# One hybrid decoder trunk on one NeuronCore: the attention loop written out as a stream of 64 steps, with projection and output projection placed inside it

## What is computed

```python
def nsa_mixer(h, pos, w_in, q_norm, k_norm, ..., w_out):
    q, k_c, v_c, k_s, v_s, k_w, v_w, g = jnp.split(h @ w_in, cuts, axis=-1)
    q = partial_rope(rms_norm(q.reshape(B, S, G, HP, dh), q_norm), pos)
...
    p_c = masked_softmax(s_c, mask_c)
    o_c = jnp.einsum('bghqc,bcgd->bqghd', p_c.astype(vc.dtype), vc)
...
    o = (gates[..., 0, :] * o_c + gates[..., 1, :] * o_s + gates[..., 2, :] * o_w).astype(h.dtype)
    return o.reshape(B, S, NSA_Q_WIDTH) @ w_out
...
    h = h + mix
    h = h + swiglu(rms_norm(h, ffn_norm_w[i]), ffn_w_gate[i], ffn_w_up[i], ffn_w_down[i])
```

## Time and profile before

| | us |
|---|---|
| median of three runs | 1614.51 (1613.33 to 1615.09) |
| the profiled execution | 1612.59 |
| its span from first to last instruction | 1610.8 |
| mean granted TensorE clock, as a share of 2.4 GHz | 0.982 |
| PE, DVE, ACT, POOL busy, share of the span | 94%, 53%, 39%, 16% |

### The profile page before, as it was taken

The page is one execution under the profiler, slowest core; times in us unless marked ns, Lnnn a source line. Parts: engine busy times, 40 slices in busy tenths (PEclk is TensorE's granted clock), DMA queues, the critical chain, the costliest instruction groups (busy, mean ns, idle before and its releaser), DMA issues.

```text
span 1610.8 us, 20549 instructions
## 1 busy us (share of the span) xinstructions
PE 1508.9 (94%) x7469; PEld 1217.9 (76%) x7469; DVE 853.7 (53%) x1137; ACT 630.9 (39%) x895; POOL 261.2 (16%) x289
## 2 busy tenths in 40 slices
PE   6989889778999999999999999998799999999999
PEld 5777667656788888788788867665687888887887
DVE  4556767663444444333397758789623444444222
ACT  4445655653343433323233352444223344343111
POOL 4133242301100000001000026666211000000000
PEclk9989999999999999999999999999799999999999
DMA  7200101102222222222222220111022222222222
GB/s 310 79 27 1 53 12 40 52 1 79 79 105 98 84 104 104 80 103 104 105 105 79 102 81 27 53 52 53 4 101 79 105 79 104 91 91 104 105 105 78
DMA packets 19198, 129.47 MB, mean 80 GB/s; under 512 B 2256, under 2 KB 2896, under 8 KB 4560
## 3 DMA queue, kind: packets, MB, share of 16 engines
q1 hardware_dynamic: 19008, 126.75, 21.9%
q10 hardware_dynamic: 144, 2.10, 0.4%
HBM read 126.74 MB, written 2.10 MB: 80 GB/s over the span
## 4 chain that ended last, share of the span: by engine, by line
PE 82%; issue 6%; DVE 5%; POOL 5%; ACT 2%; DVEq 0%; POOLq 0%; ACTq 0%
PE ps L354 22%; PE ps L356 22%; PE ps L355 22%; PE ps L624 3%; PE ps L607 2%; PE ps L772 2%; PE ps L587 2%; POOL Lx L1725 2%; POOL sqacc L1650 1%; PE ps L550 1%; PE ps L744 1%; PE ps L603 1%; PE ps L802 1%; DVE sm L1370 1%; PE ps L551 1%
## 5 line engine op out<-in xcount | busy, mean ns | idle before, releaser
L1152 DVE TENSOR_TENSOR wl<-wraw,wh 128x2048 fp32r<-128x2048 f32 x112 | 264.5, 2362 | 274.0 <-ACT wh L827 273.9
L354 PE MATMUL ps<-xh,wh 128*128 128x512 f32 (+2 forms) x912 | 359.3, 394 | 6.1 <-DVE xl L1162 3.4
L355 PE MATMUL ps<-xl,wh 128*128 128x512 f32 (+2 forms) x912 | 356.2, 391 | 0.0
L356 PE MATMUL ps<-xh,wl 128*128 128x512 f32 (+2 forms) x912 | 356.2, 391 | 0.0
L827 ACT ACTIVATE wh<-wraw 128x2048 fp32r<-128x2048 f32 x112 | 213.9, 1910 | 185.3 <-PE ps L356 175.5
L354 PEld LDWEIGHTS ps<-xh,wh 128*128 128x128 f32 (+2 forms) x912 | 170.8, 187 | 44.3 <-issue 4.5
L356 PEld LDWEIGHTS ps<-xh,wl 128*128 128x128 f32 (+2 forms) x912 | 170.7, 187 | 37.4
L355 PEld LDWEIGHTS ps<-xl,wh 128*128 128x128 f32 (+2 forms) x912 | 170.8, 187 | 37.0 <-issue 0.7
L354 PE MATMUL ps<-hh,wh 128*128 128x512 f32 x352 | 137.9, 392 | 4.1 <-DVE hid L1232 4.1
L355 PE MATMUL ps<-hl,wh 128*128 128x512 f32 x352 | 137.6, 391 | 0.0
L356 PE MATMUL ps<-hh,wl 128*128 128x512 f32 x352 | 137.5, 391 | 0.0
(11 more groups left out here) (262 smaller groups left out, 2491.1 us busy)
## 6 DMA issues: line engine op xcount, KB each, us to landing
wraw<-wstream SPq DMA_DIRECT2D x112, 1024.0 KB, 4.8
cw<-cw_in SPq DMA_DIRECT2D x1, 4096.0 KB, 18.9
xT<-xT_in SPq DMA_DIRECT2D x4, 512.0 KB, 8.1
xT<-xT_in ACTq DMA_DIRECT2D x1, 2048.0 KB, 8.5
out<-xT SPq DMA_DIRECT2D x8, 256.0 KB, 6.5
rows<-rows_in SPq DMA_DIRECT2D x1, 276.0 KB, 10.5
tri<-tri_in SPq DMA_DIRECT2D x1, 192.0 KB, 10.5
cmask<-cmask_in SPq DMA_DIRECT2D x1, 128.0 KB, 10.0
```

Of the source, the lines that this page charges most:

```text
L354: mm(o, wa[0], xa[0], start=start, stop=False)
L355: mm(o, wa[0], xa[1], start=False, stop=False)
L356: return mm(o, wa[1], xa[0], start=False, stop=stop)
L1152: TTo(wl[:, s, :], wraw[:, s, :], wh[:, s, :].bitcast(F32), ALU.subtract).then_inc(lo_done, 1)
```

## The change

The loop becomes 64 steps written out on every engine (`STEPS`, `place(S)`), without a seam between groups:

- **Lag.** `Pm` has three slots (`LAG = 3`). PE's `pT` comes three steps behind `qk`, and behind it in the step, where it was two; `pv` of a group reaches into steps 0, 1 and 3 of the next. `PT` gets a layout of its own by block.
- **Projection.** The 96 matmuls stand in steps 0 to 13 by the table `PROJECTED` (6, 2, 6, 2, 8, 3, 9, 12, 10, 6, 8, 8, 8, 8).
- **Turning keys and queries** is cut into six rounds of four transposes (`ROUND_AT`: steps 9, 11 and 14, and 0, 1 and 2 of the next group), each with its hi and lo part a step later; `kB1` and `kB2` have two copies. The rounds use the second halves of score banks and bank 7, so `qk` of steps 12 and 13 and of 0, 2 and 4 wait for their lo parts, and projection at step 0 waits for that of round 2.
- **Compressed branch.** Its scores move from k = 0 to step 5, its transposes from k = 1 and 5 to steps 6 and 9; the multiplication with the mask is folded into the gates once.
- **POOL** now makes the doubled copy of each normed tile (12 + 4 copies of 128x384) and stages the values.
- **Output projection.** Six of its eight input tiles are ready after group 2. Their 144 matmuls (`out_early`) stand in group 3 at steps 5, 7, ... 15 and 1 and 3 of the tail, one output tile of 18 matmuls each in bank 7; DVE adds each to `part`, a copy of x fetched during group 3. The other 48 matmuls take their weights from one extra chunk and follow at the end.
- **Norm of the first FFN.** `square` moves behind the residual, column sums and broadcast move into the FFN's second chunk, `split_lo(n0 + 2)` ahead of the mean.

```diff
-DVE_GROUP_STEPS, DVE_SCAN_STEPS = 26, 12
+STEPS = GROUPS * HP * TT
+LAG = 3
...
+ROUND_AT = {9: (1, 0), 11: (1, 1), 14: (1, 2), 0: (0, 3), 1: (0, 4), 2: (0, 5)}
+ROUND_BANK = (1, 3, 7, 1, 3, 1)
+
+PROJECTED = (6, 8, 14, 16, 24, 27, 36, 48, 58, 64, 72, 80, 88, 96, 96, 96)
+TILE_DONE = tuple(min(s for s in range(16) if PROJECTED[s] >= 24 * (tt + 1)) for tt in range(TT))
+TILE_READ = tuple(s + 1 for s in TILE_DONE)
...
+            def qk(S):
+
+                g, s, h, i = place(S)
+                w, par = (i + 1) * P, g % 2
+                if S >= 2:
+                    pe.wait_ge(expd, 2 * (S - 1))
+                if s in (0, 2, 4, 6):
+                    pe.wait_ge(qkT_lo, 6 * g + ((2, 3, 6, 6)[s // 2] if g else 6))
+                if g < GROUPS - 1 and s in (12, 13):
+                    pe.wait_ge(qkT_lo, 6 * (g + 1) + s - 11)
...
+            PV_AT = {10: (0, 0), 11: (0, 1), 12: (0, 2), 13: (0, 3), 15: (1, 0), 16: (1, 1), 17: (1, 2), 19: (1, 3)}
+
+            def step_of_attention(S):
+
+                g, s = divmod(S, HP * TT)
+                if S < STEPS:
+                    qk(S)
+                if LAG <= S < STEPS + LAG:
+                    pT(S - LAG)
+                if round_at(S):
+                    turn_keys_queries(*round_at(S))
+                if s in PV_AT and g < GROUPS:
+                    pv(g, *PV_AT[s])
+                if s + 16 in PV_AT and g:
+                    pv(g - 1, *PV_AT[s + 16])
+                if s == 5 and g < GROUPS:
+                    cmp_scoresT(g)
+                if g < GROUPS - 1:
+                    project(g, s)
+                if s == 6 and g < GROUPS:
+                    cmp_scores(g)
+                if s == 9 and g < GROUPS:
+                    cmp_transposes(g)
+                early = S - (STEPS - HP * TT) - 5
+                if early >= 0 and early % 2 == 0:
+                    out_early(early // 2)
...
-                for k in range(18):
-                    if k < 16:
-                        maxima(k)
-                    if 1 <= k <= 16:
-                        normalize(k - 1)
...
+            def step_of_attention(S):
+
+                g, s = divmod(S, HP * TT)
+                early = S - (STEPS - HP * TT) - 6
+                if early >= 0 and early % 2 == 0:
+                    add_part(early // 2)
+                if S < STEPS:
+                    maxima(S)
+                if s == 14 and g < GROUPS:
+                    o_rest(g, 0)
+                if s == 4 and g:
+                    o_rest(g - 1, 1)
+                if S and round_at(S - 1):
+                    round_lo(*round_at(S - 1))
+                if s == 7 and g < GROUPS:
+                    cmp_read(g)
+                if 1 <= S <= STEPS:
+                    normalize(S - 1)
+                if s == 7 and g < GROUPS:
+                    cmp_shift(g)
+                if s == 8 and g < GROUPS:
+                    cmp_probs(g)
+                if g < GROUPS - 1 and s in TILE_MEAN:
+                    qk_mean_square(TILE_MEAN.index(s), g + 1)
...
+                if g < GROUPS - 1 and s == 14:
+                    split_lo(n0 + 2 * g + 4)
+                if 1 <= g < GROUPS and s == 0:
+                    split_lo(n0 + 2 * g + 3)
...
+                pool.wait_ge(qk_rotated, g * 8 + 2 * (tt + 1))
+                pool.tensor_copy(qn[:, tt, :, 1, :], q6).then_inc(qk_normed, 1)
```

654 lines of the change are left out of this document (368 added, 286 removed).

## The result

The changed kernel takes **1590.76 us** (median of 4 runs, 1589.86 to 1595.0) where the kernel before takes 1614.8 on the same chip (1613.33 to 1615.25): a ratio of 0.9859, 95% interval 0.9847 to 0.987, or 24.0 us. I had forecast 1588.0, 26 to 27 us less. The profiled executions span 1588.0 us and 1610.8, a difference of 22.8.

What follows compares the result with a forecast made beforehand. PE, busy 94% of the span, bounds the kernel, so only its idle time can go. 46.1 us off less 21.1 of new waits, plus 1.2, gives 26.2: 1612.6 to 1586.4, the median 1.9 higher, so 1588; range 1568 to 1606.

Steps and rivals of the forecast that it cites:

- What goes off: Gains: 41.1 us of idle PE, 2 for group 3's slow clock, 3 for register instructions; 1.2 of further waiting at the end.
- Start, +2.8: Before the first qk: POOL's four copies of normed tiles lie wholly on PE's path, 2.8 us more.
- Seams, +2.2, +2.2, +4.5: Between groups: PE waits for DVE's lo parts, POOL's norm and exponentials; 2.2 us at the first two seams, 4.5 at the third.
- Within a group, +1.8 for round 1: Step 11: round 1 waits for tile 1's norm, ready 0 to 1.3 us late; 1.8 us for three groups.
- Compressed transposes, +2.3: Group 3, step 9: the compressed transposes wait for DVE's chain after a short step 8; 2.3 us.
- Empty pipe, +1.0: First steps of group 0: the pipe is empty, 1.0 us.
- FFN seam, +3.8: After the last early tile: DVE's splits and adds let the FFN's PE start 14.9 us behind it; 3.8 us more.
- Column sums, +0.5: In the FFN: POOL's eight sums of squares end at about 29.7, the column sums stand at 29.5; 0.5 us.
- (1): Rival: queues drift apart and fill better than walked, seams cost 0 to 1 us; 1572 us, chance 0.17.
- (2): Rival: the lag doesn't help, qk still waits for exponentials, groups 0 to 2 keep half their idle; 1596 us, chance 0.10.
- (3): Rival: DVE's full step 14 ends late, groups 0 to 2 keep 9.1 us idle each; 1609 us, chance 0.11.
- (4): Rival: written-out code costs PE instruction fetch in each of 64 steps; 1639 us at 0.8 a step, chance 0.08.

Runs made afterwards that it cites:

- e2: The changed kernel with the probabilities two steps behind the scores instead of three (LAG = 2): 1597.93 us.
- e12: The changed kernel with projection as 8 matmuls in each of steps 0 to 11 and a lag of two instead of three: 1593.3 us.
- e4: The changed kernel with the last group not filled: all eight early output tiles stand behind step 63, with their adds and splits: 1604.16 us.
- e6: The changed kernel with another projection table, 8 matmuls in each of steps 0 to 11 and none in 12 and 13: 1576.75 us.
- e9: The changed kernel with DVE's first weight split moved to step 13 and its second to step 1, projection in steps 2 and 3 adjusted: 1575.94 us.
- e10: The changed kernel with projection as 8 matmuls in each of steps 0 to 11 and DVE's first weight split in step 13 instead of 14: 1583.76 us.
- e5: The changed kernel with three edits behind step 63: last lo part before last early add, FFN start waiting for six tiles, squares pair by pair: 1590.22 us.
- e13: The changed kernel with DVE instead of POOL making the doubled copy of normed keys and queries, as before the change: 1582.22 us.

## Why the prediction was right, and where it wasn't

The sign and the mechanism were right, and the size within 3.4 us, in part by luck. I had 26.2 us between the spans and it is 22.8. By parts, forecast and measured: up to the first `qk` +2.8 and -0.5 (106.25 against 106.73); from there to the FFN -29.5 (46.1 and 1.2 off, 17.8 added) and -24.4; behind it +0.5 and +2.1. The middle part, which the change is about, was missed by 5.1; 3.3 at the start, which came from the clock ahead of the loop, made up for most of that, and that is luck. Behind the FFN's start PE's idle time is 0.6 us less than before and its busy time 2.7 more, with a granted clock of 0.92 in a stretch of the Mamba layer that had 0.95: that, too, is not a term of mine. Of the signs that I had named, the groups took 65.6, 67.3 and 66.0 us where I had 63 to 65, with PE idle 4.3 to 5.7 where I had 2 to 3.5; group 3 with its tail took 77.9 at 0.99 of the clock, inside its 70 to 80.

**What goes off** (46.1 and 1.2). PE's idle time in the stretch was 42.0 (316.0 less 274.0), and the old waits did go. e2 and e12 bring a wait for scaled probabilities back, e4 part of group 3's gaps; no run brings back the waits for copies and for bank 6. My 5 us for clock and registers were too much: PE's busy time fell by 2.9 only, since the seams' half clock came in new, and 20.6 us of idle time are left where I had added 17.8.

**Start, +2.8: the term was right by luck and did not show.** PE did stand 2.8 us longer ahead of the first turn (6.36 against 3.56), and POOL's copy takes 0.50, between my 0.40 and 0.83. But the four copies stretch POOL's chain by 0.57 a tile, 2.3 in all, of which DVE's last copy with its hand-off, 0.4, comes off; 0.9 is the lock again, which I had not put there: a `split_lo` holds POOL's L1843 for 2.0 us (3.00 for 0.99, at 85.21), where in the kernel before it held L1676 for 1.1 (1.91 for 0.83, at 89.43). And none of it shows at the first `qk`. PE came to this stand 1.3 us earlier than before (89.69 against 91.00), with more clock in 28 to 36 us (0.79 against 0.57). Behind it the clock, which had been at half until 103 us in the kernel before, came back at 99; the matmuls behind the turn (L774) ran in half the time, and 2.0 us of that are left at the first `qk`:

```profile
96.05 2.82 PE L591 MATMUL ps<-ident,qn 128*128 128x128 f32 x12 [6.36 <-POOL qn L1855]
...
99.30 1.95 PE L774 MATMUL ps<-cw,hidV 128*128 128x64 f32 x16
```

Most likely that is luck of the run and not of the change. In the kernels with the same start the gap is 6.4 each time, but the first `qk` comes anywhere between 105.5 and 107.9, in three of them (e4, e6, e9) behind hidV matmuls (L774, L771 in e4) of 3.62.

**Seams, +2.2, +2.2, +4.5: right place, wrong price.** The wait of 1.2 for the lo part of round 2 is there, 1.05 twice; that for exponentials at the third is there (1.76 for 2.1), those there for round 5's lo part and `o_rest(1)` (1.6 together) are not. But round 4, which I gave 0 to 1 us, waits 3.12 at each. The walk had both splits and the tile's norm in it and even said that POOL may be held; its error was to count "up to 2" where the norm meets two splits in a row (2.0 and 1.95), and to leave out the clock behind a wait of that length. In all the seams cost 13.3 us of waits (9.4, 2.1 and 1.8) and some 4 of clock (an estimate from the matmuls behind the waits at the first and third, such as L691's 2.60 at the first for 1.48 at the second), where I had 8.9. The Trainium skill's rule, "SBUF — State Buffer", "Who interferes with whom", which I had weighed as worth 2 us in all, is borne out by these runs: the later of two such ops waits for the whole of the earlier (159.51 behind 159.34, 167.32 behind 167.03, the split behind POOL in e10), and a DVE op with at most one SBUF input, outside the two-port modes, doesn't contend (the adds in e5). One SBUF input alone is no safe sign in these runs: DVE's scaling took 1.83 for 1.00 beside POOL, its copy in e13 0.73 for 0.36. What I drew from the rule was too small: one hold per seam, not two.

**Within a group, +1.8 for round 1**: no such wait. DVE was idle for 3.7 us ahead of step 14 and never so late as my walk had it. **Compressed transposes, +2.3**: 1.31. **Empty pipe, +1.0**: nothing stands there, but 1.1 in group 3's tail (L687 for the copy of probabilities) that I hadn't.

**FFN seam, +3.8**: the first matmul comes 14.0 us behind the last early tile, forecast 14.9, released by DVE's add as said. My terms for it (4.5 and 10.0) give only 14.5; the 0.4 more have no source. I missed that the last lo part stands behind `add_part` on DVE, 1.38 of PE's 14.0; but DVE has no gap over 0.2 us from 388.12 to the last add, so without this wait PE's next one, 1.46 for DVE's pair, would have been longer. **Column sums, +0.5**: 1.26. The two times of the walk, 29.7 and 29.5, differ by 0.2 and not by 0.5.

**The rivals.** (1) asked for seams without cost; that is the kernel e9 or e6, which stand at 1576 for its 1572. (2) falls: PE waits 1.8 us for exponentials in all, and the lag that it held useless is worth 7.2 us in e2 and 16.6 in e12. (3) was half true: DVE ran from 155.97 to 169.33 in step 14 to 1 without a gap of note, 13.4 us and so past my mark of 13. Its full queue cost 3.9 us of waits (2.1 and 1.8), the lock on POOL 9.4; 4 to 6 us of idle a group, not 9. (4) falls: PE shows no gap without a releaser beyond 0.2 us, but for the one before projection, which is a lo part's. The larger of the page's two instruction queues moved 0.62 MB in 38 packets, before 0.49 in 30.

What stays open: why the same wait of 3.12 us cost clock at the first and third seam and not at the second (1.00 throughout), and what each part of the loop's new order did for the waits for copies and for bank 6.

## What to carry to other kernels

When two engines lock each other out, a short op is priced by the op it can fall behind, and by how many such ops it meets; look for its neighbours on the other queue before you move it there. Moving one op of a queue moves all that stand behind it, so the collision you took away may come back one instruction later, and the same move can gain 7 us with one schedule and lose 7 with another. Spreading work evenly is no aim in itself: with slack in the pipe (here the lag of three) a compact table did as well as the spread one, and it had the work that others wait for done early.

## What the runs showed of the hardware

- A POOL copy of 128x384 from SBUF to SBUF takes 0.50 us alone and 2.45 when it began 0.29 behind a DVE `tensor_tensor` of 2.38 with both inputs in SBUF. A power over 128x6 takes 1.33 alone and 3.30 when it began 0.17 behind one of 2.29. The other way round, that `tensor_tensor` took 3.10 behind a POOL op of 1.01, and a pair of DVE lo parts 3.44 for 1.42 beside POOL sums.
- A DVE add with one input in PSUM took 0.64 beside the same POOL sums as without them. A DVE scaling of two 128x512 blocks, one input tensor in SBUF, took 1.83 beside a POOL op of 1.01 and 1.00 without, at all three seams.
- Around a stand of 3.12 us on PE the granted clock fell to 0.50 (1.2 GHz) at two seams, in 172 to 174 and in 302 to 306, and stayed at 1.00 at the one between, which stood just as long.
